# A router product in three fp32r passes on transposed rows split in two, and a single input buffer in the second stage

## The reference

```python
def grouped_moe(h, w_router, b_router, w_gate, w_up, w_down):
    ...
    scores = jax.nn.sigmoid((xt @ w_router).astype(jnp.float32))
    sel = (scores + b_router.astype(jnp.float32)).reshape(T, N_GROUPS, EXPERTS_PER_GROUP)
    group_score = lax.top_k(sel, TOP_K)[0].sum(-1)
    group = jnp.argmax(group_score, axis=-1)
    in_group = jnp.take_along_axis(sel, group[:, None, None], axis=1)[:, 0]
    _, local = lax.top_k(in_group, TOP_K)
    expert_idx = group[:, None] * EXPERTS_PER_GROUP + local
    gate = jnp.take_along_axis(scores, expert_idx, axis=1)
    gate = gate / gate.sum(-1, keepdims=True)
    ...
        hb = jax.nn.silu(xb @ w_gate[e]) * (xb @ w_up[e])
        return hb @ w_down[e]
    ...

def reference(...):
        y = fourier_mixer(x, fourier_w_in[j], fourier_w_out[j])
        x = layer_norm(DEEPNORM_ALPHA * x + y, ln_g[i, 0], ln_b[i, 0])
        y = grouped_moe(x, router_w, router_b, expert_w_gate[i], expert_w_up[i], expert_w_down[i])
        x = layer_norm(DEEPNORM_ALPHA * x + y, ln_g[i, 1], ln_b[i, 1])
```

## Time and profile before

| what | us |
|---|---|
| median of 3 runs | 2231.27 |
| lowest and highest | 2230.52, 2238.21 |
| the profiled execution | 2227.85 |
| its span | 2225.8 |
| TensorE busy in the span | 2069.3 (93%) |
| VectorE busy | 1385.2 (62%) |
| ScalarE busy | 953.7 (43%) |
| POOL busy | 581.8 (26%) |

### The profile page before, as it was taken

One profiled execution on the slowest core, in us unless ns is written; L12 is line 12 of the kernel. 1 busy time (PEld: TensorE's weight loads), 2 busy tenths in 40 slices (PEclk: granted clock), 3 DMA queues, 4 the chain that ended last, 5 costly groups with the idle time before them and its releaser, 6 DMA issues.

```text
span 2225.8 us, 38714 instructions
## 1 busy us (share of the span) xinstructions
PE 2069.3 (93%) x12300; PEld 1793.4 (81%) x12301; DVE 1385.2 (62%) x2339; ACT 953.7 (43%) x1446; POOL 581.8 (26%) x600
## 2 busy tenths in 40 slices
PE   7989899999999739999999999999999999999990
PEld 4557778888788539899899899998999999989980
DVE  4342347776876857666666676676666666666644
ACT  2231121221222315554555555555555555555534
POOL 3000023433433522322232222222222323223214
PEclk9999999999999959999999999999999999999995
DMA  5896233343432447877687787888877978878836
GB/s 201 281 297 150 92 137 135 128 146 116 149 125 95 152 153 246 249 213 227 208 259 243 212 258 232 229 258 256 234 232 219 260 228 237 263 230 243 244 71 207
DMA packets 149488, 451.38 MB, mean 203 GB/s; under 512 B 43488, under 2 KB 45536, under 8 KB 145248
## 3 DMA queue, kind: packets, MB, share of 16 engines
q1 hardware_dynamic: 98592, 277.59, 39.3%
q0 software_dynamic: 50848, 173.14, 26.5%
HBM read 337.50 MB, written 117.78 MB: 205 GB/s over the span
## 4 chain that ended last, share of the span: by engine, by line
PE 88%; issue 5%; DMA 3%; DVE 2%; ACT 1%; SPq 1%; ACTq 0%; POOLq 0%; POOL 0%; DVEq 0%
PE ps L961 36%; PE ps L989 16%; PE ps L821 16%; PE ps L765 3%; PE ps L949 3%; PE ps L806 3%; PE ps L997 3%; PE ps L862 2%; DMA xch<-x 2%; PE ps L779 2%; PE ps L731 1%; PE ps L849 1%; PE ps L954 1%; DVE fin_r L1709 1%; PE ps L817 1%
## 5 line engine op out<-in xcount | busy, mean ns | idle before, releaser
L989 PE MATMUL ps<-wd_hi,hidT 128*128 128x512 f32 x1056 | 293.0, 402 | 0.4 <-ACT hidT L1212 0.4
L1494 DVE TENSOR_TENSOR wd_lo<-wraw,wd_hi 128x1024 fp32r<-128x1024 f32 x132 | 161.7, 1225 | 158.3 <-ACT wd_hi L1165 152.4
L989 PEld LDWEIGHTS ps<-wd_hi,hidT 128*128 128x128 f32 x1056 | 190.0, 188 | 36.3 <-ACT hidT L1212 0.8
L1494 DVE TENSOR_TENSOR wu_lo<-wraw,wu_hi 128x1024 fp32r<-128x1024 f32 x132 | 160.7, 1218 | 53.3 <-ACT wu_hi L1165 48.2
L961 PE MATMUL ps<-mxT_hi,wg_hi 128*128 128x256 f32 (+2 forms) x1056 | 163.5, 298 | 29.1 <-issue 28.7
L961 PEld LDWEIGHTS ps<-mxT_hi,wg_hi 128*128 128x128 f32 x1056 | 146.0, 193 | 42.3 <-issue 35.5
L1115 ACT CAST xt_hi<-ps 128x256 fp32r<-128x256 f32 x128 | 41.4, 375 | 323.2 <-PE ps L806 323.2
L1494 DVE TENSOR_TENSOR wg_lo<-wraw,wg_hi 128x1024 fp32r<-128x1024 f32 x132 | 161.1, 1222 | 29.1 <-ACT wg_hi L1165 25.6
L1850 POOL DMA_INDIRECT sums<-yrow_a,ent_now x33 | 58.3, 1766 | 416.3 <-DVE yrow_a L1570 359.1
L961 PE MATMUL ps<-mxT_lo,wg_hi 128*128 128x256 f32 (+2 forms) x1056 | 159.1, 294 | 0.0
L961 PE MATMUL ps<-mxT_hi,wg_lo 128*128 128x256 f32 (+2 forms) x1056 | 157.9, 292 | 0.0
(11 more groups left out here) (265 smaller groups left out, 4100.4 us busy)
## 6 DMA issues: line engine op xcount, KB each, us to landing
wraw<-expert_w_gate SPq DMA_DIRECT2D x132, 512.0 KB
wraw<-expert_w_up SPq DMA_DIRECT2D x132, 512.0 KB, 5.0
wraw<-expert_w_down SPq DMA_DIRECT2D x132, 512.0 KB, 4.4
xch<-x SPq DMA_DIRECT2D x16, 1024.0 KB, 9.1
first_stage<-ych SPq DMA_DIRECT2D x16, 1024.0 KB, 10.5
yt<-first_stage SPq DMA_DIRECT2D x16, 1024.0 KB
w_out_s<-fourier_w_out SPq DMA_DIRECT2D x4, 1024.0 KB, 9.2
w_in_s<-fourier_w_in SPq DMA_DIRECT2D x1, 4096.0 KB, 21.8
```

Of the source, the lines that this page charges most:

```text
L989: mm = nc.tensor.matmul(psY[h], hidT[:, l, c, t * P:(t + 1) * P], wd[r][:, c, cols], start=(i == c == 0), stop=(i == 2 and c == FC - 1))
L1494: nc.vector.tensor_tensor(piece(1, j), wraw[:, j % SLOTS, :], piece(0, j).bitcast(F32), ALU.subtract).then_inc(wlo_ok, 1)
```

## The change

The transposed rows are kept in two parts: ScalarE writes the high part (fp32r), VectorE subtracts it from the bank and writes the low part (`turn_lo`). The router weight is split in the same way once, into a stationary operand of 64 columns (32 of the high part, 32 of the low part). The router product of group g-2 stands between the halves of group g's cross product: 8 chunks by 2 parts of the rows, in fp32r, into 64 rows of scores. The scores are copied, and the product that transposes them uses two stacked unit matrices (`halves`), which adds the two parts; the sigmoid comes behind it. `yt` and `m2s` have one buffer, whose second place holds the rows' low part. Three small operations take the place of one in the table of LayerNorm tiles.

```diff
-        yt_t = at("yt", 144, 4 * D)
+        yt_t = at("yt", 144, 2 * D)
-        hT_t = at("hT", 176, 2 * D)
+        hT_t = [at("hT_hi", 176, 2 * D, F32R), at("hT_lo", 152, 2 * D, F32R)]
...
             def load_group(g, b):
-                sp.wait_ge(xj_ps, s2_base(g - 2) + 4)
+                sp.wait_ge(xj_ps, s2_base(g - 1) + 4)
...
@@ second_stage
                     if jj < 2 and not is_first(g, 3):
-                        pe.wait_ge(xj_ev, base_j - 1 + jj)
+                        pe.wait_ge(th_lo, 4 * g - 9 + jj)
...
@@ turn_rows
                         if last:
-                            pe.wait_ge(xj_ev, base_j + max(jj - 1, 0))
+                            pe.wait_ge(th_lo, 4 * g + max(jj - 1, 0))
                         elif jj < 3:
                             pe.wait_ge(xj_ev, base_j - 2 + jj)
                             pe.wait_ge(xl_ev, 4 * g + 10 + jj)
                         else:
-                            pe.wait_ge(xj_ev, base_j + 1)
+                            pe.wait_ge(th_lo, 4 * g + 1)
...
-            def router(g, base_j, dst=psL):
...
+            def router(g, dst=psL):
                 for c in range(CH):
                     if c % 4 == 0:
-                        pe.wait_ge(xj_ev, base_j + 2 + c // 2)
-                    mm = nc.tensor.matmul(dst, rwv[:, c, :], hT[:, c, :, :].rearrange("p s n -> p (s n)"),
-                                          start=(c == 0), stop=(c == CH - 1))
+                        pe.wait_ge(th_lo, 4 * g + 2 + c // 2)
+                    for r in range(2):
+                        mm = nc.tensor.matmul(dst, rw2[:, c, :, :].rearrange("p r e -> p (r e)"),
+                                              hT[r][:, c, :, :].rearrange("p s n -> p (s n)"),
+                                              start=(c == r == 0), stop=(r == 1 and c == CH - 1))
                 mm.then_inc(lg_ps, 1)
...
@@ turn_scores
-                    mm = nc.tensor.transpose(dst[:, s * E:(s + 1) * E], scT[:, s * P:(s + 1) * P],
-                                             ident[0:E, 0:E])
+                    mm = nc.tensor.matmul(dst[:, s * E:(s + 1) * E], scT[:, s * P:(s + 1) * P],
+                                          halves[0:2 * E, :], start=True, stop=True)
...
+            def cross_product(g):
+                if not is_first(g):
+                    pe.wait_ge(q_ev, g)
+                product_half(psQ, 1, B, 0, is_first(g))
+                if not is_first(g, 2):
+                    router(g - 2)
+                product_half(psQ, 1, B, 1, is_first(g)).then_inc(q_ps, 1)
...
@@ group of the tensor engine
                 if not is_first(g):
                     turn_rows(g - 1, 1 - b, tr_base(g))
-                    router(g - 1, tr_base(g))
...
@@ the last group of the tensor engine
             turn_rows(g - 1, 0, tr_base(g))
-            router(g - 1, tr_base(g), psL2)
+            pe.wait_ge(p_ev, g)
+            product_half(psP, 0, A, 0, passes=range(2))
+            router(g - 1, psL2)
+            product_half(psP, 0, A, 0, passes=range(2, 3))
             ranks(g - 2)
-            pe.wait_ge(p_ev, g)
-            product_half(psP, 0, A, 0)
...
@@ the scalar engine
+            def scores(g, b):
                 act.wait_ge(lg_ps, g + 1)
...
+                nc.scalar.copy(scT, psL2 if second else psL).then_inc(sg_ok, 1)
+                act.wait_ge(st_ps, g + 1)
+                nc.scalar.activation(sc2[b].rearrange("p s e -> p (s e)"), psS2 if second else psS, ACT.Sigmoid
+                                     ).then_inc(sc_ok, 1)
...
@@ the vector engine
+            def turn_lo(g, base_j):
+                for jj in range(4):
+                    dve.wait_ge(xj_ev, base_j + jj + 1)
+                    nc.vector.tensor_tensor(hT_dst(1, jj), hT_src(g, jj), hT_dst(0, jj).bitcast(F32), ALU.subtract
+                                            ).then_inc(th_lo, 1)
...
                 rows_cross(g, b, i)
+                if not is_first(g):
+                    turn_lo(g - 1, tr_base(g))
                 rows_ready(g, b)
...
@@ the last group of the vector engine
             rows_cross(g, 1, GROUPS // 2 - 1)
-            choose(g - 2)
+            choose(g - 2, 1)
+            turn_lo(g - 1, tr_base(g))
             take_ranks(g - 2)
             place(g - 2, 1, GROUPS // 2 - 2)
-            choose(g - 1, psS2)
+            choose(g - 1, 0)
             rows_ready(g, 1)
             rows_finish(g, 1)
             take_ranks(g - 1, psR2)
+            turn_lo(g, tr_base(GROUPS))
             place(g - 1, 0, GROUPS // 2 - 1)
```

More of the change, by code:

```diff
@@ L104, in shape_constants @@
     parts = [("f1", f1), ("ident", np.eye(P)), ("before", before), ("ones", np.ones((P, P))),
[L105 removed]
+             ("cs", cs), ("halves", np.tile(np.eye(E), (P // E, 1))), ("first", first), ("firstg", firstg),
              ("ebase", ebase), ("ustep", ustep), ("unit", unit), ("expert", expert)]
@@ L271, in trunk_kernel @@
         grow = Row(192, 200)
-        m2s, rw = grow.take("m2s", 2 * 2 * P), grow.take("rw", CH * E)
+        m2s, rw = grow.take("m2s", 2 * P), grow.take("rw", CH * E)
+        rw2 = grow.take("rw2", CH * 2 * E, F32R).rearrange("p (c r e) -> p c r e", c=CH, r=2)
         def chunks(name, kib, n):
@@ L331, in trunk_kernel @@
         payg = [grow.take(f"payg{b}", 12, I32) for b in range(2)]
-        scT = grow.take("scT", 2 * P)[0:E, :]
-        sc, sel, sel2, eq = (small(n, 2, E) for n in ("sc", "sel", "sel2", "eq"))
+        scT = grow.take("scT", 2 * P)[0:2 * E, :]
+        sc2, sel, sel2, eq = [small("sc0", 2, E), small("sc1", 2, E)], *(
+            small(n, 2, E) for n in ("sel", "sel2", "eq"))
         rank, msum = (small(n, 2, LISTS) for n in ("rank", "msum"))
@@ L415, in trunk_kernel @@
         dve_gate, pool_gate, pe_gate = sem("dve_gate"), sem("pool_gate"), sem("pe_gate")
+        th_lo, sc_ok, rw_hi, rw_lo = (sem(n) for n in ("th_lo", "sc_ok", "rw_hi", "rw_lo"))
         edge_ok, edge_read, edge_zero = sem("edge_ok"), sem("edge_read"), sem("edge_zero")
@@ L494, in last_bank, with hT_src, hT_dst @@
             return psX[1 + jj % 2]
+        def hT_src(g, jj):
+            last = isinstance(g, int) and g >= GROUPS - 2
+            return (last_bank if last else turn_bank)(jj).rearrange("p (c n) -> p c n", c=4)
+        def hT_dst(part, jj):
+            return hT[part][:, 4 * (jj // 2):4 * (jj // 2) + 4, jj % 2, :]
         def s2_src(jj):
@@ L806, in second_stage, with product_half @@
                             mm = nc.tensor.matmul(s2_bank(jj)[:, lo:lo + P],
-                                                  yt[:, b, q, cc * P:(cc + 1) * P],
-                                                  m2t[:, b, q, :], start=True, stop=True)
+                                                  yt[:, q, cc * P:(cc + 1) * P],
+                                                  m2t[:, q, :], start=True, stop=True)
                     mm.then_inc(xj_ps, 1)
-            def product_half(ps, m, w, h, edge_row=False):
+            def product_half(ps, m, w, h, edge_row=False, passes=range(3)):
                 cols = slice(h * HALF, (h + 1) * HALF)
@@ L818, in product_half @@
                                              start=(n == 0 and c == 0), stop=False)
-                for n, (l, r) in enumerate(PASSES):
+                for n in passes:
+                    l, r = PASSES[n]
                     for c in range(CH):
@@ L824, in product_half @@
                 return mm
[L826 to L830, removed]
             def turn_rows(g, b, base_j):
@@ L920, in _ @@
             turn_rows(g, 1, tr_base(GROUPS))
-            router(g, tr_base(GROUPS))
+            router(g)
             turn_scores(g)
@@ L1122, in empty_turn @@
                         act.wait_ge(lg_ps, g)
-                    hh = jj // 2
-                    last = isinstance(g, int) and g >= GROUPS - 2
-                    src = (last_bank if last else turn_bank)(jj)
-                    nc.scalar.copy(hT[:, 4 * hh:4 * hh + 4, jj % 2, :],
-                                   src.rearrange("p (c n) -> p c n", c=4)).then_inc(xj_ev, 1)
-            def scores(g):
-                act.wait_ge(lg_ps, g + 1)
-                if not is_first(g):
-                    act.wait_ge(st_ps, g)
-                src = psL2 if isinstance(g, int) and g == GROUPS - 2 else psL
-                nc.scalar.activation(scT, src, ACT.Sigmoid).then_inc(sg_ok, 1)
+                    nc.scalar.copy(hT_dst(0, jj), hT_src(g, jj)).then_inc(xj_ev, 1)
+            def scores(g, b):
+                act.wait_ge(lg_ps, g + 1)
+                second = isinstance(g, int) and g == GROUPS - 2
+                nc.scalar.copy(scT, psL2 if second else psL).then_inc(sg_ok, 1)
+                act.wait_ge(st_ps, g + 1)
+                nc.scalar.activation(sc2[b].rearrange("p s e -> p (s e)"), psS2 if second else psS, ACT.Sigmoid
+                                     ).then_inc(sc_ok, 1)
             def group(g, b, last=False):
```

(17 more changed lines are left out.)

45 lines of the change are left out of this document (25 added, 20 removed).

## The result

The changed kernel takes 2271.1 us, median of four runs (2268.79 to 2277.12), against 2231.98 for the kernel before (2230.52 to 2238.21, four runs). The ratio is 1.0168, with a 95% interval of 1.015 to 1.0186: slower, by 39 us. The profiled execution took 2268.79 us with a span of 2266.8; before, 2227.85 and 2225.8.

What follows compares the result with a forecast made beforehand. It took TensorE, busy throughout the second stage's loop, as the bound. -1.1 + 21.8 + 11.3 + 7.5 + 2.0 = +41.5 us on 2227.85 gave 2269.4, or 2272.8 on the median; it gave 2271 us, range 2250 to 2294.

Steps and rivals of the forecast that it cites:

- The wait: Loop: TensorE's fourth block of transposes waits for VectorE's first subtraction, which comes after rows_cross; 2.9 us idle each period.
- The period: Loop, groups 2 to 15: each period 34.17 us against 32.49, +1.68 us 13 times, +21.8 us.
- Group 1: No router or ranks there; group 2's cross product starts at 301.12 instead of 302.25, -1.1 us.
- The clock: TensorE's clock falls after some of the loop's idle stretches, 2.3 us each; +7.5 us in the loop.
- one fall in four: Loop: assumed rate of clock falls, one in four periods, 13 x 2.3 / 4 = +7.5 us.
- The tail: From group 15 on: rows_ready(15) +9.0 us, subtractions ahead of place(14) +2.3; +11.3 in all, plus +2.0 for the clock.
- The lower bound: Tail: +3 us instead of +11.3, if code fetches, which are in the 4.66 us, fell elsewhere.
- What hid: Loop edits costed at nothing, among them the single buffer of yt and ScalarE's extra copy and 64-column sigmoid.
- The sum: Whole kernel: group 2's earlier start, loop, tail and clock terms add to +41.5 us; 2271 us given.
- The chances: Own case 68%, clock falling every period 15%, narrow products no faster 7%, only cross banks binding 6%; slower 92%.
- The third rival: Loop: only the freeing of the cross banks binds, not the fourth block; period 33.0 us, 2243 us; chance 6%.
- The rule of the Trainium skill: Rival: in the loop the clock falls in every period, 30 us instead of 7.5; 2295 us on the median; chance 15%.

Runs made afterwards that it cites:

- cross_first: Changed kernel with one edit in VectorE's order, rows_cross(g) ahead of empty_s2(g+1); 2226.99 us, ratio to the kernel before 0.9982.
- filled_gap: Changed kernel with 11 small f32 products on constants in TensorE's gap ahead of the fourth block of transposes, groups 2 to 14; 2263.25 us, ratio 1.0145.
- first_block_early: Changed kernel with only the first of VectorE's four subtractions moved ahead of rows_cross; 2266.65 us, ratio to the kernel before 1.0149.
- both: Changed kernel with rows_cross ahead of empty_s2 and, in the last groups, group 14's subtractions ahead of choose(13); 2224.81 us, ratio 0.9958.
- one_buffer: Kernel before with only the single buffer of yt and m2s, loads one group later; 2234.35 us, ratio 1.0013.
- no_split: Changed kernel without the split: old f32 router product in the new place, no subtractions, score transposes as before; 2267.94 us, ratio 1.016.

## Why the prediction was right

It gave 2271 and 2271.1 was measured. Step by step, on the profiled executions:

- **The wait.** Right in its place, its releaser and its size: fourth block, VectorE's first subtraction, 2.76 to 2.88 us where 2.9 was reckoned. `cross_first` shows that it is the cause, since an order of VectorE that changes no work takes 36 us out of the 13 periods.
- **The period.** 34.17 reckoned; periods without a fall lie between 33.8 and 34.3, 34.0 in the mean, so the 13 cost 19.6 us over the kernel before and not 21.8. The router took 1.82 us, not 1.94 (0.114 us for each narrow product against 0.121); the turning of the scores 0.56 us, not 0.44. The two errors cancel. TensorE went on 0.74 us after the subtraction's start (610.09 - 609.35), where 0.83 was reckoned.
- **Group 1.** -1.1 reckoned, -1.2 measured.
- **The clock.** 7.5 us reckoned for the loop; 5.3 for three falls by `filled_gap`, and 6.3 in all (448.34 less 13 times 34.0) with the one that reached in from group 1. The guess of one fall in four was near, but by luck: it rested on one idle stretch of 3.25 us that had passed at full clock, and in the changed kernel's trace the clock fell in that same stretch (158.61, in the 3.29 us ahead of 159.20). `first_block_early` had six falls with less idle time.
- **The tail.** +11.3 and +2.0 for the clock; +13.8 measured (`rows_ready(15)` +10.9 where 9.0 and 2.0 stood). The 2.0 can be seen: behind the wait of 8.79 us the 16 products at 772.21 take 5.88 us, where 3.9 is usual. `both` confirms the wait of the third block behind `choose(13)`, and that it is only part of the tail: 71.40 us remain against 63.59. How much of that is the new order of the passes, no run shows alone. The lower bound spoke of code fetches in the 4.66 us ahead of 749.00; the trace has instruction loads starting at 731.30 and 754.59 and none in between, so that remark has no row behind it.
- **What hid.** The single buffer cost nothing (`one_buffer`). Nothing in ScalarE's new order held TensorE: the only wait of the loop is the one named.
- **The sum.** The three stretches that the working covers moved by 38.6 us against 41.5 reckoned: -1.2 for -1.1, 19.6 for 21.8, 6.3 for 7.5, and 13.8 for 13.3. The remaining gap to the measured 40.9 of the profiled executions is luck outside them: -2.2 ahead of the second stage and +4.6 behind the tail. Some of the hit is therefore chance; the error of the working is 3 us. The chances also have a slip that changes nothing: 68, 15, 7 and half of 6 make 93% for slower, not 92.

The third rival (only the cross banks bind) fell, as the two waits are in the order that the text gave; `first_block_early` shows it as the next one in line, with 33.6 us. The rule of the Trainium skill, "TensorE: Matmul & The Clock Gate", section "HAM oscillation — how this bites in real kernels", that each burst behind a wait of some microseconds starts slow, held for 3 of 13 periods here. The loop that the section describes has longer waits than the 2.8 us of this one, so the two don't contradict each other; that every gap of this size costs a fall is what the measurement rules out.

## What to carry to other kernels

When a piece of work is moved off the end of a period, ask what it covered there: here 3.57 us of TensorE's work hid a chain of VectorE that needed 1.8 of them, and moving it alone (`no_split`) cost 2.1 us a period, though it gave TensorE nothing more to compute. A wait on an engine that is idle elsewhere in the same period is a question of order, not of speed: look for a step in its program whose input is ready long before its place. And once a wait is taken away, look for the next one close behind it.

## What the runs showed of the hardware

The granted clock falls over gaps much shorter than I had thought safe. In first_block_early it fell six times in 13 periods with idle stretches of 0.61 and 1.69 us, in no_split three times with a single one of 1.80 to 1.91; in cross_first, with 0.60, never. How often it falls doesn't follow the length of the gap alone: the changed kernel, with 2.8 us, had three. Transposes stand directly ahead of all these gaps (1.97 us of them in no_split, 1.51 in the others), and no run separates their part from that of the idle time. Nor does one trace foretell the next: the same idle stretch of the first stage passed at full clock before (3.25 us ahead of 162.54) and held a fall in the changed kernel's trace (3.29 us ahead of 159.20). These counts are from one execution each.

The falls of the changed kernel lasted 3.4 or 6.8 us and cost a period between 0.9 and 2.7 us (34.9 and 36.7 against 34.0). Useless products in the gap kept the clock at 2.4 GHz and were worth 5.3 us of the loop.
